# The work area of a two-layer trunk kernel starts 128 bytes lower in on-chip memory

## The reference, cut to what matters

```python
def swiglu(h, w_gate, w_up, w_down):
    return (jax.nn.silu(h @ w_gate) * (h @ w_up)) @ w_down

# even layer
h = rmsnorm(x, norm_mix)
q, k, v, z, xbc, dt = split_cols(h @ w_in, [A_WIDTH] * 3 + [B_WIDTH, B_CONV_CH, B_HEADS])
...
x = x + jnp.concatenate([y_a, y_b], axis=-1) @ w_out
return x + swiglu(rmsnorm(x, norm_ffn), w_gate, w_up, w_down)

# odd layer
x = x + jnp.concatenate([y_c, y_d], axis=-1) @ w_out
return x + moe_swiglu(rmsnorm(x, norm_ffn), router, e_gate, e_up, e_down)
```

## Time and profile before

| | |
|---|---|
| median of 3 runs | 2368.44 us (2365.76 to 2368.75) |
| the profiled execution, its own time | 2369.58 us |
| its span in the trace | 2367.6 us |
| PE busy | 2241.0 us, 95% of the span |
| DVE, ACT, POOL busy | 49%, 40%, 5% |
| mean granted TensorE clock | 0.980 of full speed |
| moved by the transfers | 451.15 MB, mean 191 GB/s |

### The profile page before, as it was taken

One profiled execution on the slowest core, in us unless ns is written; L12 is line 12 of the kernel. 1 busy time (PEld: TensorE's weight loads), 2 busy tenths in 40 slices (PEclk: granted clock), 3 DMA queues, 4 the chain that ended last, 5 costly groups with the idle time before them and its releaser, 6 DMA issues.

```text
span 2367.6 us, 37773 instructions
## 1 busy us (share of the span) xinstructions
PE 2241.0 (95%) x15391; PEld 1927.3 (81%) x15391; DVE 1166.1 (49%) x1567; ACT 941.8 (40%) x1176; POOL 120.5 (5%) x181
## 2 busy tenths in 40 slices
PE   7998999999999888989899999999999998999995
PEld 6864988888888677649687888888789998999995
DVE  3267533323254678473688888888883000000001
ACT  4247432222242444374367677776772000000001
POOL 6101000000000000000000000010100000000000
PEclk9999999999999999999899999999999999999998
DMA  6320233232322000110799999999989768768663
GB/s 198 113 81 9 72 107 98 98 130 98 98 88 68 2 3 3 37 36 14 280 365 346 386 349 380 350 370 356 372 325 312 258 215 281 259 214 294 225 226 106
DMA packets 262115, 451.15 MB, mean 191 GB/s; under 512 B 8359, under 2 KB 148494, under 8 KB 261854
## 3 DMA queue, kind: packets, MB, share of 16 engines
q1 hardware_dynamic: 257216, 435.73, 52.5%
q0 software_dynamic: 4576, 13.41, 2.3%
q10 hardware_dynamic: 190, 0.05, 0.0%
HBM read 436.63 MB, written 12.52 MB: 190 GB/s over the span
## 4 chain that ended last, share of the span: by engine, by line
PE 86%; DVE 6%; ACT 4%; issue 2%; DMA 1%; ACTq 0%; DVEq 0%; POOLq 0%; SPq 0%; POOL 0%
PE bank L712 83%; PE bank L715 3%; DVE arena L2133 2%; DVE w_low L2133 1%; DVE slot L2133 1%; ACT w_high L2051 1%; ACT arena L1661 0%; ACT arena L1762 0%; ACT arena L1670 0%; DMA xs<-sum_rows_d 0%; ACT arena L1638 0%; DMA sum_rows_d<-arena,idx_now 0%; ACT w_high L1606 0%; DMA vec_rows<-in_b_norm_w_dram 0%; DVE arena L2887 0%
## 5 line engine op out<-in xcount | busy, mean ns | idle before, releaser
L2133 DVE TENSOR_TENSOR w_low<-slot,w_high 128x2048 fp32r<-128x2048 f32 x172 | 393.5, 2291 | 311.1 <-ACT w_high L1606 250.3
L712 PE MATMUL bank<-arena 128*128 128x144 f32 (+6 forms) x2672 | 344.9, 299 | 6.1 <-DVE small L2292 2.5
L712 PEld LDWEIGHTS bank<-arena 128*128 128x128 f32 (+4 forms) x2672 | 312.5, 183 | 21.2 <-issue 9.6
L712 PE MATMUL bank<-arena,slot 128*128 128x144 f32 (+4 forms) x2368 | 310.5, 301 | 9.8 <-issue 5.2
L2133 DVE TENSOR_TENSOR arena<-arena,bank 128x512 f32<-128x512 f32 (+2 forms) x99 | 58.7, 593 | 525.0 <-PE bank L712 525.0
L712 PEld LDWEIGHTS bank<-arena,slot 128*128 128x128 f32 (+2 forms) x2368 | 287.1, 183 | 29.3 <-issue 22.4
L2133 DVE TENSOR_TENSOR w_low<-arena,w_high 128x2048 fp32r<-128x2048 f32 x105 | 239.5, 2289 | 23.4 <-ACT w_high L2051 22.8
L712 PE MATMUL bank<-w_high,xg_high 128*128 128x512 f32 x560 | 225.0, 402 | 7.2 <-DVE w_low L2133 5.1
L2051 ACT ACTIVATE w_high<-slot 128x2048 fp32r<-128x2048 f32 x108 | 206.2, 1915 | 64.3 <-PE bank L712 38.1
L2051 ACT ACTIVATE w_high<-arena 128x2048 fp32r<-128x2048 f32 x105 | 201.0, 1919 | 58.6 <-PE bank L712 58.5
L712 PE MATMUL bank<-h_ffn,w_high 128*128 128x512 f32 (+1 forms) x736 | 218.6, 380 | 0.8 <-DVE w_low L2133 0.8
(11 more groups left out here) (373 smaller groups left out, 3252.4 us busy)
## 6 DMA issues: line engine op xcount, KB each, us to landing
slot<-in_moe_w_up_dram SPq DMA_DIRECT2D x86, 1024.0 KB, 6.1
arena<-in_moe_w_gate_dram SPq DMA_DIRECT2D x78, 1024.0 KB, 6.3
arena<-in_moe_w_down_dram SPq DMA_DIRECT2D x64, 1024.0 KB, 5.4
slot<-in_moe_w_down_dram SPq DMA_DIRECT2D x48, 1024.0 KB, 5.5
slot<-in_moe_w_gate_dram SPq DMA_DIRECT2D x34, 1024.0 KB, 5.1
arena<-in_moe_w_up_dram SPq DMA_DIRECT2D x26, 1024.0 KB, 5.7
slot<-in_e_w_in_dram SPq DMA_DIRECT2D x12, 1024.0 KB, 5.4
slot<-in_ff_w_gate_dram SPq DMA_DIRECT2D x11, 1024.0 KB, 5.3
```

The costliest lines, as they stand in the source:

```text
L712: return pe.matmul(o, lhsT, rhs, start=start, stop=True, skip_group_check=True)
L2133: return dve.tensor_tensor(o, a, b, op)
```

## The change

The filler ahead of the arena shrinks from 192 to 64 bytes. The arena starts at byte 105,792 of each partition in place of 105,920, at remainder 64 on division by 256 in place of 192. All that lies in the arena moves along, the rounded tensors that are placed by `arena_at` included. Slots, `xs` and the small tensors stay where they are. No instruction, size, wait or order changes.

```diff
-        sb("arena_shift", [P, 48])
+        sb("arena_shift", [P, 16])
         ARENA = 30600
         arena = sb("arena", [P, ARENA])
         arena_at = nc.sbuf_base - 4 * ARENA
```

## The result

| | before | changed |
|---|---|---|
| median of 4 runs, us | 2367.7 (2365.76 to 2368.75) | 2388.45 (2385.55 to 2389.78) |
| ratio, 95% interval | | 1.0088 [1.0076, 1.01] |
| profiled execution: own time, span, us | 2369.58, 2367.6 | 2385.55, 2383.4 |

The changed kernel is 20.8 us slower. The profiled execution of before took longer than any of its four runs, and the one after is the fastest of its four, so these two lie only 16.0 us apart. The text says which pair it uses.

A forecast was written before the change was run, and what follows sets the result against it. PE was taken to bound the kernel (86% of the span). All four terms were 0 (0 + 0 + 0 + 0), leaving the median of 2368.4 us; the range was 2354 to 2398 us.

The forecast's parts named there:

- ACT and DVE at 0: Tile instructions touching the arena: 1 ns each at most, nothing on the path since both wait for PE; 0.
- the transfers at 0: Split turns' transfers into the arena: 0.5 us quicker or slower each, still 0 on the path.
- plain float32 at 0: Last three turns: rows 672 bytes apart already meet weights at many remainders, yet 124.6 ns a matmul holds; 0.
- rival C: Split turns: arena transfers get quicker or slower; 2363 us at best, likely no change; chance only pooled with others.
- the term of the split products: Dense layers and split turns: matmuls going from 0 to 128 bytes apart keep their rhythm of 128 bytes; 0.
- The witness against the loss: Dense 160-column tile: blocks alternately 0 and 128 apart take 0.34 and 0.33 us, speaking against 6.5 ns a matmul.
- A: Split products: unit is 256 bytes and 128 apart is good, 2.5 ns a matmul, 13.7 us gained, 2354.7 us; chance 0.26.
- B: Split products: 128 apart locks into the slow rhythm, 6.5 ns a dense matmul; 33.9 us, 2402 us; chance 0.29.
- The witness for 64 apart: Second output projection, pieces 6 and 7: operands 64 bytes apart take 117.5 ns a matmul against 120.0 at 0.
- the slow stretch of the earlier trace: Split turns before the change: after a pause, ten matmuls of a tile came every 233.0 ns, against 227.5 elsewhere.
- only the 512-column matmuls: Smaller loss price: 2256 dense matmuls caught, 14.7 us, plus 9.2 in the split turns; 24 us, 2392 us.
- The signs that were named: Changed profile, dense SwiGLU: 226 to 227 ns for no change, some 224 for a gain, 231 to 233 for a loss.

The follow-up runs named there:

- the version that beats both: Against the kernel before, weight halves lie 64 bytes lower in dense stages where 256 weight columns move: 2363.04 us against 2367.08, ratio 0.9982.
- the blocks: At "gave 117.8": kernel computing nothing of the reference, only 48-matmul blocks on PE at eight operand distances; 256 columns, 192 apart: 117.8 ns per matmul.

## Why the prediction was wrong, point by point

Forecast was no change, 2368.4 us; it became 2388.45.

**ACT and DVE at 0, the transfers at 0, plain float32 at 0: right.** 2292 and 2291 ns again; the kernel with only the raw slots moved is at ratio 1.0; 11.96 us for 96 plain matmuls again. The prediction's reason for the last, that rows 672 bytes apart meet at many remainders and still agree, was right in its result, and the four distances run by themselves give 122.5 ns a record each. The transfers' small change in landing reached nobody, as argued; rival C is out.

**What failed is the term of the split products.** The step was: "The excess of 13.3 ns is 32 cycles at 2.4 GHz ... 32 cycles of a float32 stream are 128 bytes. I read it as a start that waits for a rhythm of 128 bytes, which a shift by exactly 128 bytes leaves as it was." In its place the runs showed that a distance of 128 is not like 0: 232.1 ns against 226.7 with PE alone, while 256 is as 0 and 384 as 128. In the kernel the term put at 0 measured 6.1 ns for each of 2256 dense 512-column matmuls, 13.9 us, and 7.3 us in the split turns. That two lengths agree was a coincidence of numbers read as a mechanism; the same 13.3 ns would have fitted any story with 32 cycles in it. The prediction said itself that it fails if the unit is 256. Its statement that all 3794 dense matmuls go from 0 to 128 apart is also not exact: `y_high_odd` 6 and 7 went from 64 to 192, and the 160-column blocks had both distances before and after. Few matmuls are concerned, and no price hangs on it.

**The witness against the loss didn't testify.** The 160-column blocks stood alternately at 0 and 128 and showed no difference, and this was counted against both A and B. They are at 111.3 ns in both kernels. The prediction had noted that here the weight load sets the pace and then used the blocks twice all the same. A pair of places where something else is the limit says nothing about the limit's neighbour.

**The witness for 64 apart was read too widely.** 117.5 beside 120.0 ns is real, but it holds for 256 columns, and from it A took 2.5 ns for 512 columns as well. There 64 apart costs 6.6 ns. And pieces 6 and 7, which were to keep their 117.5 ns, went to an irregular 116.7 on average: their 24 matmuls run from 1089.97 to 1092.77 us in the changed trace.

**Rival B was right that 128 apart is the bad distance**, and its size: 232 to 234 ns on average, like the slow stretch of the earlier trace rows. That the pair is locked into that same rhythm isn't shown. The intervals of the earlier trace rows scatter from 224 to 240 ns and come back to 226 and 227 within the next tile, at distance 0; those at 128 apart alternate between 229 and 238 in the stretch of the dense SwiGLU shown, and nowhere in the dense layers do they come back. Of its two prices the one for "only the 512-column matmuls" was the nearer, 24 us and 2392. The measured terms: dense 13.9 us where 14.7 was estimated; split turns 8.3 us where 9.2 was; and one term that it didn't have, −1.4 us for the 256-column ones. The split turns passed on 7.3 of their 8.3 us, since PE set their pace.

**The signs that were named** came out as for B: 231 to 233 ns in the dense SwiGLU (233.8 in the stretch shown, 232.9 in the mean), the third tiles nearly unchanged (228.0 to 228.9) while the others slowed. One did not: B wanted the output projection above 120.0, and it went to 118.75.

**What stays open.** Why PE needs 6 ns more at these distances isn't shown. The runs exclude other engines, the place within 256 bytes (at 512 columns), and a cost in proportion to the columns loaded. The distance isn't the only thing that picks the rhythm: narrow stationary operands slow down even at distance 0, and at 256 columns one distance gives several intervals. The v tiles of the first input projection have 64 bytes between their operands in two kernels and take (77.02 − 74.98) / 18 = 113.3 ns with the arena at remainder 0 and (77.30 − 74.83) / 21 = 117.6 in the version that beats both. With the arena at 128 the second output projection, 192 apart, has stretches at 113.3 ns, where the blocks gave 117.8. Between such kernels the buffers also lie apart by other multiples of 256 bytes, which no run varied by itself; what else decides was not found.

## What to carry to other kernels

When buffers feed both operands of fp32r matmuls with 512 moving columns, look at their distance modulo 256 bytes and not at either address: an unused filler of some bytes between two buffers was worth 0.9% of this kernel. Where a trace has the same operation at two such distances, compare them only where the operation's own stream sets the pace, and at the same width: 64 apart was good at 256 columns and bad at 512, and at 256 columns the distance alone didn't fix the interval. A reading of a constant ("13 ns are 32 cycles are 128 bytes") is no evidence until a second row, at another distance, agrees with it.

## What the runs showed of the hardware that was not expected

- The interval of fp32r matmuls with 512 moving and 128 stationary columns is 226.7 ns when the operands start at the same remainder of 256 bytes and 228.9 to 234.1 ns otherwise, with PE working alone. With 256 moving columns it is 120.0 ns at the same remainder and 113.3 to 120.0 otherwise, and one distance can give either 113.3 or 117.8.
- At 512 columns the distance has a direction: stationary 64 bytes above moving gives 233.3 ns, 64 below (192 above) 228.9 ns.
- Plain float32 matmuls with 144 columns are recorded as two, 122.5 ns from one record to the next, at every distance tried.
- PE's busy time hides this: in the split turns it was 619.8 us of 625 before and 618.8 after the earlier trace rows. The start-to-start time, or the same piece of the chain in both traces, shows it.
